# Who squares the rows of x at the start of a block kernel with mLSTM and dilated attention

## The reference, cut to what matters

```python
def rmsnorm(x, w):
    xf = x.astype(jnp.float32)
    y = xf * lax.rsqrt(jnp.mean(xf * xf, axis=-1, keepdims=True) + NORM_EPS) * w.astype(jnp.float32)
    return y.astype(x.dtype)

def hybrid_layer(x, pre_w, w_in, ...):       # x: 1 x 1024 tokens x 1024 features, f32
    h = rmsnorm(x, pre_w)
    proj = h @ w_in                          # 1024 x 12296: all queries, keys, values and gates
    ...                                      # causal convolution, chunkwise mLSTM, three dilated attentions
    merged = sigmoid(g_m) * branch_m + sigmoid(g_a) * branch_a
    return x + rmsnorm(merged @ w_out, post_w)
```

## Time and profile before

| | us |
|---|---|
| median of three runs | 1371.04 (1370.8 to 1371.63) |
| the profiled execution's own time | 1369.94 |
| its span on the core | 1368.1 |
| PE busy in the span | 1352.3 (99%) |
| DVE busy | 794.5 (58%) |
| ACT busy | 641.7 (47%) |
| POOL busy | 569.2 (42%) |
| mean granted TensorE clock | 0.998 of full |

### The profile page before, as it was taken

One profiled execution on the slowest core, in us unless ns is written; L12 is line 12 of the kernel. 1 busy time (PEld: TensorE's weight loads), 2 busy tenths in 40 slices (PEclk: granted clock), 3 DMA queues, 4 the chain that ended last, 5 costly groups with the idle time before them and its releaser, 6 DMA issues.

```text
span 1368.1 us, 18779 instructions
## 1 busy us (share of the span) xinstructions
PE 1352.3 (99%) x6470; PEld 1127.3 (82%) x6470; DVE 794.5 (58%) x1260; ACT 641.7 (47%) x1320; POOL 569.2 (42%) x400
## 2 busy tenths in 40 slices
PE   7999999999999999999999999999999999999998
PEld 5788888888888888888888888888888888888786
DVE  5874438346543835877756575755644442997632
ACT  6644543543444455345445445544544553533421
POOL 5253435335443534654434445344333544454000
PEclk9999999999999999999999999999999999999999
DMA  6132233324233323455442634345343354966421
GB/s 194 51 76 65 69 74 90 96 48 126 76 85 72 84 79 61 149 173 144 114 145 66 188 104 134 100 127 175 87 150 97 93 188 165 345 200 196 183 97 58
DMA packets 210462, 165.02 MB, mean 121 GB/s; under 512 B 32400, under 2 KB 186544, under 8 KB 210368
## 3 DMA queue, kind: packets, MB, share of 16 engines
q1 hardware_dynamic: 210224, 163.75, 40.5%
q10 hardware_dynamic: 144, 0.07, 0.0%
HBM read 117.41 MB, written 40.08 MB: 115 GB/s over the span
## 4 chain that ended last, share of the span: by engine, by line
PE 91%; DVE 4%; issue 2%; ACT 1%; DMA 1%; SPq 1%; POOL 0%; DVEq 0%; POOLq 0%; ACTq 0%
PE proj L1244 69%; PE side L1189 3%; PE proj L1189 2%; PE side L1289 2%; PE side L1268 2%; PE side L1345 2%; PE side L1354 2%; PE proj L1170 2%; PE side L1170 2%; PE side L1277 1%; PE side L1317 1%; PE side L1350 1%; PE side L1300 1%; DMA x_sb<-x_in 1%; PE side L1362 1%
## 5 line engine op out<-in xcount | busy, mean ns | idle before, releaser
L1080 POOL TENSOR_TENSOR w_lo<-raw,w_hi 128x512 fp32r<-128x512 f32 x161 | 234.5, 1458 | 413.8 <-ACT w_hi L1456 413.7
L1244 PE MATMUL proj<-hi_T,w_hi 128*128 128x512 f32 x832 | 338.1, 406 | 2.2 <-ACT snap L1474 1.6
L1244 PE MATMUL proj<-hi_T,w_lo 128*128 128x512 f32 x832 | 325.2, 391 | 0.0
L1244 PE MATMUL proj<-lo_T,w_hi 128*128 128x512 f32 x832 | 324.1, 390 | 0.0
L1244 PE MATMUL proj<-hi_B,w_hi 128*128 128x512 f32 x624 | 254.1, 407 | 5.6 <-ACT b_sb L1518 4.0
L1244 PE MATMUL proj<-hi_B,w_lo 128*128 128x512 f32 x624 | 244.2, 391 | 0.0
L1244 PE MATMUL proj<-lo_B,w_hi 128*128 128x512 f32 x624 | 243.6, 390 | 0.0
L1080 POOL TENSOR_TENSOR w_lo<-s_sb,w_hi 128x512 fp32r<-128x512 f32 x104 | 156.7, 1510 | 153.5 <-ACT w_hi L1456 153.4
L1244 PEld LDWEIGHTS proj<-hi_T,w_hi 128*128 128x128 f32 x832 | 156.4, 188 | 36.0 <-issue 3.5
L1244 PEld LDWEIGHTS proj<-hi_T,w_lo 128*128 128x128 f32 x832 | 156.1, 188 | 34.2
L1244 PEld LDWEIGHTS proj<-lo_T,w_hi 128*128 128x128 f32 x832 | 156.6, 188 | 30.4
(11 more groups left out here) (253 smaller groups left out, 2014.5 us busy)
## 6 DMA issues: line engine op xcount, KB each, us to landing
raw<-w_in SPq DMA_DIRECT2D x95, 512.0 KB, 6.0
m_spill<-stage SPq DMA_DIRECT2D x16, 1024.0 KB, 5.6
chunk<-m_spill SPq DMA_DIRECT2D x32, 512.0 KB, 3.8
gate_spill<-stage SPq DMA_DIRECT2D x8, 1024.0 KB, 4.3
gst<-gate_spill SPq DMA_DIRECT2D x32, 256.0 KB, 3.2
share<-share_spill SPq DMA_DIRECT2D x12, 512.0 KB, 5.0
x_sb<-x_in SPq DMA_DIRECT2D x8, 512.0 KB, 7.6
hm_spill<-stage SPq DMA_DIRECT2D x4, 1024.0 KB, 8.8
```

The source lines that it names most:

```text
L1080: TT(w_lo_ring[k % RING][:], src, w_hi_ring[k % RING][:].bitcast(F32), ALU.subtract).then_inc(lo_pool, 1)
L1244: mm = pe.matmul(acc(p, which), w[:, kt, :], m[:, kt, :], start=(first and kt == 0 and w is wh and m is h_hi[b]), stop=(kt == 3 and w is w ...
```

## The change: what it does

All eight tiles are squared by ScalarE; `late_square` and its semaphore go. Tile 5 is now scaled by VectorE like tile 4 and turned by transposes; only 6 and 7 go through diagonals. Squares 4 to 7 stand between ScalarE's high parts, and the copy of bank 1 stands behind the last square. On VectorE the scaling of tiles 4 and 5 stands between the low parts, and the first two `second_half` steps stand ahead of the low part of `iw`. On GpSimd `low(0)` stands ahead of the root of tile 4.

```diff
@@ gpsimd
             def reciprocal_root(t):
-                if t < 5:
-                    g.wait_ge(x_ms, t + 1)
-                else:
-                    g.wait_ge(x_sq_late, t - 4)
+                g.wait_ge(x_ms, t + 1)
...
             for t in range(4):
                 reciprocal_root(t)
+            low(0)
             reciprocal_root(4)
-            low(0)
             low(1)
+            reciprocal_root(5)
             g.wait_ge(ident_in, 16)
-            for t in range(5, NT):
+            for t in range(6, NT):
                 diagonal(t)
@@ tensor, second_half
-                    if t == 0:
-                        pe.wait_ge(x_scaled, 5)
+                    if t < 2:
+                        pe.wait_ge(x_scaled, 5 + t)
                     else:
-                        pe.wait_ge(x_norm, t)
+                        pe.wait_ge(x_norm, t - 1)
...
-                    if t == 0:
+                    if t < 2:
                         mm = pe.transpose(columns, turned, ident[:])
                     else:
                         mm = pe.matmul(columns, turned, diag[:, 4 + t, :], start=True, stop=True)
@@ scalar
             high(0)
-            square(4)
             act.wait_ge(start_in, 16 * NSTART)
             first_high(0)
             first_high(1)
+            square(4)
             first_copy(0)
             first_high(2)
             first_high(3)
-            first_copy(1)
+            square(5)
             first_high(4)
             high(1)
-            for kt in range(5, KT):
-                first_high(kt)
+            first_high(5)
+            square(6)
+            first_high(6)
+            first_high(7)
+            square(7)
+            first_copy(1)
             for kt in COPY_ORDER[2:]:
                 first_copy(kt)
@@ vector
-            def late_square(t):
...
-            for t in range(5):
+            for t in range(4):
                 mean_square(t)
                 scale(t)
-            for kt in range(4):
+            for kt in range(3):
                 first_low(kt)
-            late_square(5)
+            mean_square(4)
+            first_low(3)
+            scale(4)
             first_low(4)
-            late_square(6)
+            mean_square(5)
             first_low(5)
-            late_square(7)
+            scale(5)
+            mean_square(6)
             first_low(6)
             first_low(7)
+            mean_square(7)
+            for j in range(2):
+                second_half(j)
             dve.wait_ge(iw_hi_done, 1)
             for c in range(2):
                 ins = TT(iw[:, :, 2 + c:P:32], ifw[:, :, c * MH:(c + 1) * MH], iw[:, :, c:P:32].bitcast(F32), ALU.subtract)
             ins.then_inc(iw_lo_done, 1)
-            for j in range(4):
+            for j in range(2, 4):
                 second_half(j)
```

More of the change, by code:

```diff
@@ L611, in hybrid_kernel @@
         v_step = sem("v_step")
-        x_ms, x_sq_late, x_scaled = sem("x_ms"), sem("x_sq_late"), sem("x_scaled")
+        x_ms, x_scaled = sem("x_ms"), sem("x_scaled")
         iw_lo_done = sem("iw_lo_done")
```

## The result

The changed kernel takes 1372.8 us (median of 20 runs, 1371.66 to 1376.92) against 1370.81 us for the kernel before in the same series: ratio 1.0020, 95% interval 1.0013 to 1.0027. By the medians it is 2.0 us slower. The ratio and its interval are worked out over all fast runs, and are not the ratio of the two medians; of the 20 runs of the kernel before, two took 2320.59 and 3541.6 us and stay out of it. In us the interval is +1.8 to +3.7. The forecast was +1.0, called no change; the time lies inside the range, but the slowing is beyond what the measurement leaves open, twice what I had worked out.

The account below looks back on a forecast made before the run. TensorE, busy 99% of 1368.1 us, bounds the kernel; early on it runs just behind ScalarE and VectorE. P2's end +0.25 at full clock, low clock +1.43, second half -0.70 give +1.0: median 1372.0, range 1369.5 to 1373.0.

Parts of the forecast that it names:

- VectorE's `iw` behind the second_half steps: VectorE, after the critical copy: the moved `iw` pair costs nothing, covered by the second half's saved 0.7 us; otherwise 0.3.
- Scale of tile 3: VectorE's scale(3) stands behind GpSimd's low(0), taking 1.74 us instead of 0.75; term 0 or +0.99, taken as +0.99.
- the rival: scale(3) goes first, ScalarE's list 0.99 us earlier: 1371.0 with slow P2 (chance 0.22), 1369.6 with fast (0.10).
- ScalarE's list: ScalarE from first_high(0) at 13.46 to the copy of bank 1 at 23.35: 9.89 us; P2 may begin at 24.09.
- P1: TensorE's first product begins at 16.40, 0.83 us earlier, but gains nothing since P2 waits for bank 1; taken at full clock.
- VectorE without its squares: VectorE in P2: 4.1 us of squares and 1.6 us of stalls go; P2 runs without a stall.
- Clock: TensorE stands 3.5 to 4.9 us ahead of P2, so P2 runs at low clock: 4.18 us, +1.43 over full clock.
- rival of a longer low clock: Low clock lasts into TensorE's second half: +7.2 us, 1378; half of it +3 to +4; chance 0.06.
- Second half: TensorE's feature tiles take 0.67 us each instead of 0.78, first tile's 0.26 wait goes; -0.70 in the sum.
- critical copy: ScalarE's copy released by TensorE's fourth turned feature tile; its start, called s, moves from 30.18 to 31.15, +1.0 us.
- its own sign of being wrong: Beyond 55 us the prediction expected the same work shifted by one amount; anything else would show it wrong.

Follow-up runs that it names:

- e6: The changed kernel with the low part of `iw` made by one VectorE instruction instead of two, at the same place: 1372.08 us, ratio 1.0010.
- e7: The changed kernel with filler matmuls of zeros in P1 and the low part of `iw` back at its old place: 1370.02 us, ratio 0.9994.
- e8: The kernel before, with only VectorE's first two second_half steps moved ahead of the low part of `iw`: 1371.88 us, ratio 1.0007.
- e5: The changed kernel itself, measured again in a later series against the kernel before: 1373.36 us, ratio 1.0018.
- e4: The changed kernel with three matmuls of zeros added into P1's sum to keep TensorE at work: 1371.48 us, ratio 1.0006.
- e1: The changed kernel with the low part of `iw` back ahead of all VectorE's second_half steps: 1372.21 us, ratio 1.0012.
- e9: The changed kernel with GpSimd's low(0) held until tile 3 is scaled: 1373.77 us, ratio 1.0021.
- e10: The changed kernel with the DMA of the first weights issued ahead of x tile 3 instead of tile 4: 1374.26 us, ratio 1.0029.

## Why the prediction was wrong

**The step that failed** is "VectorE's `iw` behind the second_half steps": "So this edit costs nothing". I had the meeting with low(2) right (32.33 = s + 1.29, `iw` at s + 1.58) and priced it by the old 1.40 us, as one stand for the pair. That row was a lucky case. Before, GpSimd had 0.17 us between its two sums, and the second narrow instruction slipped into the gap (it began at 28.5 and took 0.21):

```profile
27.23 1.27 POOL L1068 TENSOR_TENSOR s_sb<-raw 128x512 f32<-128x512 f32 x1
28.67 1.28 POOL L1074 TENSOR_TENSOR s_sb<-s_sb,raw 128x512 f32<-128x512 f32 x1 [0.17 <-POOL s_sb L1068]
```

In the new place low(2) and the low parts of T2 follow each other without one, so each of the two instructions stood: 2.28 us. T2(2) moved from s + 3.37 to s + 4.62 instead of my s + 3.36, the gate product waited 1.33 instead of 0.27. That is +1.25 on the path, shown by the profiles of e6, e7 and e8.

The other terms, in the prediction's order:

- *Scale of tile 3.* Mechanism right, outcome open: it took 1.75 us in three (e5, e6, e7) of the nine profiles in which the changed order was left to itself, and 0.75 in the other six. In the profile after, the first weights' high part ended at 12.00 instead of 11.20, so scale(3) went first, as the rival had it. What I had not seen is the next gate: first_high(0) then waited for `ifw` to land and began at 13.23, 0.23 before my 13.46 and not 0.99. Two misses nearly cancelled.
- *ScalarE's list*: 9.83 us from first_high(0) to the copy of bank 1 (13.23 to 23.06), forecast 9.89. P2 began at 23.84, forecast 24.09.
- *P1*: gains nothing, right. But I took it fast, and it ran mostly at the low clock (16.8 to 20.2). So TensorE stood 3.07 us ahead of P2, less than my 3.5 to 4.9.
- *VectorE without its squares*: P2 ran without a stall, right; the additions did not stand behind GpSimd (0.14 to 0.15 us each).
- *Clock*: P2 took 4.34 us, forecast 4.18; e4 confirms the size (1.45 and 1.43). The premise was weaker than the result: I had the clock hold for 3.5 us without work, from one row. It fell 2.8 us into the stand here, 2.0 in e1, 2.1 in e9, and in e6, after a stand of 2.19, when P2 was half done. That the term came out right with a stand of 3.07 has some luck in it. Nor is the low level in a run one number: P2 was slow for its first half (after), for all of it (e1, 5.3 us), for all but its last two matmuls (e9, 4.9 us), or for its later part (e6 from 25.7, 4.0 us). Over the 31 runs of the changed kernel in two series, those with a mean clock of 0.997 average 1372.7 us, 0.996 1373.7, 0.995 1374.8; the profile after is the fastest of its series. My rival of a longer low clock was priced as one rare case of +7 us, or +3 to +4 for half of it; two of the profiles (e1, e9) have a longer one that costs 0.5 to 0.9 us of P2. That it makes the longer runs is a correlation of run means, which also count P1, where the low clock costs nothing; no profile of a run of the changed kernel near 1375 was taken.
- *Second half*: pitch 0.66 against 0.67 forecast, and no wait for a diagonal; right.

The critical copy was thus forecast within 0.11 us, and T2(2) missed by 1.15. Of the shift, 0.4 us is given back between 57 and 1300 us, which I did not follow and the forecast had at nothing (its own sign of being wrong, that the rest beyond 55 us is not shifted by one amount). So the whole of the profiled execution is +1.72 where T2(2) is +2.11.

**Left open:** why e1 gained only 0.2 to 0.7 us by the median where its profile shows the full 1.2, and why e9 gained nothing. A longer low clock, as in both profiles, would do it, but it was seen in one execution of each. There is a second candidate that has nothing to do with the change: behind 57 us the shift grows in both (e1 from T2(2) +1.78 to +2.62 at the first output DMA, e9 from +2.45 to +2.99), as it does in e6 (+1.41 to +4.10). In these three TensorE waits 0.5 us for ScalarE's `prob` near 361 us, in e6 also 0.9 us for VectorE's `gst` near 1179; the profiles of before and after have neither of these two waits. How often this happens in runs that were not profiled is not known.

## What to carry to other kernels

When an instruction of one engine is priced from a row in which it stood behind another engine, look at what follows on that other engine: a short gap there may be why a second instruction did not stand as well. Count the stands by instructions, not by the work in them (2.28 us for two, 1.12 for one with the same elements), and where the place can't be changed, make one instruction of two. And where work is moved onto an engine with free time, ask which semaphore its list frees next: here not the squares but one copy behind them held TensorE, long enough for its clock to fall.

## What the runs showed of the hardware that was not expected

A VectorE subtraction of 32 elements per partition took 0.21 us alone and up to 1.30 us behind a GpSimd instruction. It has two inputs from SBUF; the low parts from PSUM with one (0.74 us) ran beside GpSimd's low(1) at their usual length, and so did the one-column additions. This is the case that the Trainium skill names (GPSIMD Engine Reference, Key points: contention with two SBUF inputs); the trace agrees, with 1.06 to 1.30 us for such an instruction against 0.21 alone, and shows that the stand lasts until GpSimd's instruction is done. Two inputs are not the whole of it: the scaling of a tile has one tensor as input and stood too (1.75 us against 0.75). What sets it apart from the additions no run here shows.

The clock can fall in the midst of work. In e6 TensorE stood from 22.0 to 24.18, ran P2 at full clock for 1.5 us, and was at 0.50 from 25.7 to 29.1, with no stand in between. e10 shows the same (P2 from 25.52 at full clock, 0.50 from 26.8, after a stand of 2.18). The windows of e6 (granted clock the last column but two):

```profile
25.00:26.00 1.00, 1.00 (x5) 0.83 (x4) 0.00 (x0) 1.00 (x3) 1.00 (x2) 0.85 0.00 0
26.00:27.00 1.00, 1.00 (x4) 0.76 (x3) 0.00 (x0) 1.00 (x3) 0.83 (x2) 0.50 0.00 0
...
29.00:30.00 1.00, 1.00 (x11) 1.00 (x10) 0.49 (x1) 0.00 (x0) 0.00 (x0) 0.94 0.00 0
```
